# LayerNorm of the mix by thirds: tiles centred as they arrive, statistics on 88 rows, last mix tiles and first feed-forward products by thirds

## What is computed

```python
mix = (g_conv * y_conv + g_mla * y_mla) @ p['w_mix_out']
x1 = _layer_norm(DN_ALPHA * x + mix, p['ln1_g'], p['ln1_b'])
h, ffn_state = _causal_dwconv(ffn_prev, x1 @ p['w_up'], p['ffn_dw_w'], p['ffn_dw_b'])
hg, hv = jnp.split(h, 2, axis=-1)
f = (jax.nn.silu(hg) * hv) @ p['w_down']
y = _layer_norm(DN_ALPHA * x1 + f, p['ln2_g'], p['ln2_b'])
```

## Time and profile before

| | us |
|---|---|
| median of 3 runs | 2294.15 (2285.85 to 2295.95) |
| time of the profiled execution | 2278.77 |
| its span in the trace | 2276.9 |
| mean clock that TensorE was granted in it | 0.953 of full |
| TensorE busy | 2101.8 (92% of the span) |
| VectorE, ScalarE, GpSimd busy | 1324.0, 654.0, 443.0 |
| HBM traffic | 76 GB/s over the span |

### The profile page before, as it was taken

The page is one execution under the profiler, slowest core; times in us unless marked ns, Lnnn a source line. Parts: engine busy times, 40 slices in busy tenths (PEclk is TensorE's granted clock), DMA queues, the critical chain, the costliest instruction groups (busy, mean ns, idle before and its releaser), DMA issues.

```text
span 2276.9 us, 34903 instructions
## 1 busy us (share of the span) xinstructions
PE 2101.8 (92%) x13705; PEld 1989.7 (87%) x13705; DVE 1324.0 (58%) x1743; ACT 654.0 (29%) x1066; POOL 443.0 (19%) x230
## 2 busy tenths in 40 slices
PE   5999999969989999979989996799999999999992
PEld 5999999958979888866659995699999999999992
DVE  4799999964536666634433324855444454454545
ACT  3221222135224444433422102522222222222212
POOL 2222221101100010033311221121221222212213
PEclk6999999989979999989988997899999999999995
DMA  7222222215310000045624431011111111111102
GB/s 222 66 60 72 75 65 66 85 46 176 124 41 13 12 23 12 19 187 222 260 107 132 122 102 47 19 56 38 52 46 40 46 37 56 47 37 47 46 27 99
DMA packets 161092, 173.64 MB, mean 76 GB/s; under 512 B 19564, under 2 KB 136102, under 8 KB 156852
## 3 DMA queue, kind: packets, MB, share of 16 engines
q1 hardware_dynamic: 142805, 97.63, 14.6%
q0 software_dynamic: 8368, 46.27, 5.3%
q10 hardware_dynamic: 9825, 28.48, 3.4%
HBM read 145.48 MB, written 27.73 MB: 76 GB/s over the span
## 4 chain that ended last, share of the span: by engine, by line
PE 68%; issue 15%; DVE 12%; ACT 3%; DMA 1%; ACTq 1%; POOL 0%; DVEq 0%; POOLq 0%; SPq 0%
PE psb L1753 18%; PE psa L1753 18%; PE psb L2188 6%; PE psa L2188 6%; PE psb L1862 5%; PE psa L1862 4%; DVE pst L1262 4%; PE psb L2088 1%; PE pst L2067 1%; DMA xt_d<-xst 1%; PE psa L2035 1%; PE psb L2035 1%; PE pst L1932 1%; DVE ptl L1411 1%; PE psb L1767 1%
## 5 line engine op out<-in xcount | busy, mean ns | idle before, releaser
L1262 DVE SCALAR_TENSOR_TENSOR pst<-g_ext,wtap,pst 128x512 f32<-128x512 f32 x464 | 306.9, 745 | 0.0
L1179 POOL TENSOR_TENSOR wlo<-wraw,whi 128x1024 fp32r<-128x1024 f32 x64 | 173.3, 2720 | 637.8 <-ACT whi L1046 637.8
L1643 DVE TENSOR_SCALAR hg<-ueg,fwv,vec 128x1024 f32<-128x1024 f32 x22 | 17.9, 813 | 231.1 <-ACT ueg L1063 231.1
L1115 POOL TENSOR_TENSOR wlo<-wraw,whi 128x1024 fp32r<-128x1024 f32 x32 | 77.0, 2412 | 377.6 <-ACT whi L648 358.3
L1753 PE MATMUL psa<-x1h,whi 128*128 128x352 f32 x528 | 115.9, 328 | 18.2 <-DVE x1l L1618 16.6
L1121 POOL TENSOR_TENSOR wlo<-wraw,whi 128x1024 fp32r<-128x1024 f32 x32 | 77.3, 2417 | 270.4 <-ACT whi L682 270.3
L1753 PE MATMUL psa<-x1h,wlo 128*128 128x352 f32 x528 | 114.2, 324 | 0.0
L1753 PE MATMUL psb<-x1h,whi 128*128 128x352 f32 x528 | 114.2, 324 | 0.0
L1753 PE MATMUL psa<-x1l,whi 128*128 128x352 f32 x528 | 114.1, 324 | 0.0
L1753 PE MATMUL psb<-x1h,wlo 128*128 128x352 f32 x528 | 113.8, 323 | 0.0
L1753 PE MATMUL psb<-x1l,whi 128*128 128x352 f32 x528 | 113.7, 323 | 0.0
(11 more groups left out here) (423 smaller groups left out, 5245.2 us busy)
## 6 DMA issues: line engine op xcount, KB each, us to landing
wraw<-in_w_up SPq DMA_DIRECT2D x44, 512.0 KB, 3.7
wraw<-in_w_in SPq DMA_DIRECT2D x37, 512.0 KB, 3.8
wraw<-in_w_down SPq DMA_DIRECT2D x22, 512.0 KB, 3.5
gb_d<-stg ACTq DMA_DIRECT2D x8, 528.0 KB, 2.7
ga_d<-stg ACTq DMA_DIRECT2D x8, 528.0 KB, 2.7
gab<-ga_d ACTq DMA_DIRECT2D x8, 528.0 KB, 4.4
ma_d<-stg ACTq DMA_DIRECT2D x8, 528.0 KB, 2.9
tmp<-gb_d SPq DMA_DIRECT2D x8, 528.0 KB, 3.7
```

Of the source, the lines that this page charges most:

```text
L1115: nc.gpsimd.tensor_tensor(wlo[:, n % HL, :], wraw[:, n % RAW, :], whi[:, n % HL, :].bitcast(F32), ALU.subtract).then_inc(lo_done, 1)
L1179: nc.gpsimd.tensor_tensor(wlo[:, (ns + 2) % HL, :], wraw[:, (ns + 2) % RAW, :], whi[:, (ns + 2) % HL, :].bitcast(F32), ALU.subtract).then_ ...
L1262: half[x] = link(nc.vector.scalar_tensor_tensor(out=dst, in0=src, scalar=tap(k_), in1=pst[:, x, :], op0=ALU.mult, op1=ALU.add))
```

## The change

The LayerNorm of the mix is worked in another order:

- Behind mix1, VectorE adds `res` tiles 0 and 1 (`pair`); behind mix2, TensorE sums that over the partitions in three parts, ScalarE scales by 1/256. This shift, the mean of two tiles, is taken off every tile: for tiles 2 to 7 VectorE forms alpha * x - shift in `stg` before the mix tile is there (`shifted`), and the add out of PSUM then gives the centred tile. Sums (`s1`) and squares (`tmp`) are added up tile by tile; ScalarE's squares stand between its casts of weights.
- The 44 transposes of state rows move behind mix3.
- mix6 and mix7 are made by thirds of the tokens, 24 matmuls each, in the order 6, 7, 6, 7, 6, 7 (`third`).
- Statistics per third: `token_sums` makes 16 FP32 matmuls with the data as weights (128 x 88) and one column of ones, so that sum and square sum of 352 tokens lie on 88 partitions x 4 columns. VectorE and ScalarE compute mean, variance, root, reciprocal on 88 x 4. `spread` brings 1/sd and -mean/sd back to all partitions with 8 FP32 matmuls against the identity. The first two thirds' sums and spreads stand inside the thirds of mix6 and mix7, the third spread behind the first third of GATE0 and VAL0.
- Normalising is a multiply and an add on VectorE per tile and third; then gain, bias, high and low part as before, by thirds.
- GATE0 and VAL0 are made by thirds (`first_up`): per third, GATE0 then VAL0, first the 16 matmuls with the high activations, then the 8 with the low ones.
- On ScalarE the casts of the weights of GATE1 and VAL1 move in front of the last third. The scaling of `res` by alpha moves behind the convolutions of GATE0 (tiles 0 to 3) and VAL0 (tiles 4 to 7).

SyncE's order is not changed.

```diff
-            for m in range(MT):
+            for m in range(3):
                 hi(N4 + m + 2)
...
+            for c in range(3):
+                act.wait_ge(l1_p, PS[f"c{c}"])
+                step(f"c{c}", nc.scalar.activation(stat[:, part3(c)], pst[:, c % 2, 0:CH], ACT.Copy, scale=1.0 / (2 * P)))
+            for m in range(2):
+                act.wait_ge(l1_v, VS[f"d{m}"])
+                step(f"sq{m}", nc.scalar.activation(tmp[m][:, :], res[:, m, :], ACT.Square))
+            for m in range(2, 6):
+                hi(N4 + m + 3)
+                mixed(m)
+                act.wait_ge(l1_v, VS[f"q{m - 1}"])
+                step(f"sq{m}", nc.scalar.activation(tmp[0][:, :], res[:, m, :], ACT.Square))
...
+            hi(N5 + 1)
+            square(6, 0)
+            square(7, 0)
+            sums_root(0)
+            square(6, 1)
+            spread(0)
...
+            affine(1, 0)
+            affine(1, 1)
+            spread(2)
...
+            for k in range(2, MT):
+                affine(1, k)
+            for kind in (GATE0, VAL0):
+                ffn_hi("first", kind)
+            for k in range(MT):
+                affine(2, k)
...
+            def shifted(m):
+                dve.wait_ge(xt_in[m % 2], 16 * (m // 2 + 1))
+                step(f"y{m}", nc.vector.scalar_tensor_tensor(out=stg[m % 2][:, :], in0=stg[m % 2][:, :], scalar=ALPHA,
+                                                             in1=stat[:, :], op0=ALU.mult, op1=ALU.subtract))
...
+            for m in range(2, 6):
+                q, n = ring[f"mix{m}"]
+                dve.wait_ge(w_used, N4 + m + HL + 1)
+                dve.wait_ge(l1_v, VS[f"y{m}"])
+                nc.vector.tensor_tensor(split(res[:, m, :]), split(stg[m % 2][:, :]), acc(q), ALU.add).then_inc(free[q], 1)
+                mixed(m)
+                step(f"p{m}", nc.vector.tensor_tensor(s1[:, :], s1[:, :], res[:, m, :], ALU.add))
+                dve.wait_ge(l1_s, AS[f"sq{m}"])
+                step(f"q{m}", nc.vector.tensor_tensor(tmp[1][:, :], tmp[1][:, :], tmp[0][:, :], ALU.add))
+                shifted(m + 2)
...
+            def normalise(c, k):
+                x = res[:, k, part3(c)]
+                if k == 0:
+                    dve.wait_ge(l1_s, AS[f"br{c}"])
+                step(f"u{c}{k}", nc.vector.tensor_tensor(x, x, stat[:, part3(c)], ALU.mult))
+                dve.wait_ge(l1_v, VS[f"u{c}{k}"])
+                step(f"n{c}{k}", nc.vector.tensor_tensor(x, x, s1[:, part3(c)], ALU.add))
...
+            for c in (1, 2):
+                for k in range(MT):
+                    normalise(c, k)
+                    if k:
+                        low(c, k - 1)
+                low(c, MT - 1)
...
+            def token_sums(c):
...
+                for kind, parts in enumerate(((s1[:, :], res[:, 7, :]), (tmp[1][:, :], stg[1][:, :]))):
+                    for x in range(SUB):
+                        cols = slice(c * CH + x * ST, c * CH + (x + 1) * ST)
+                        for k, src in enumerate(parts):
+                            last = nc.tensor.matmul(pst[0:ST, 0, 480 + kind * SUB + x:481 + kind * SUB + x], src[:, cols],
+                                                    ones[:, 0:1], start=k == 0, stop=k == 1)
...
+            between = {(6, 1): (token_sums, 0), (7, 1): (spread, 0), (6, 2): (token_sums, 1), (7, 2): (spread, 1)}
+            for c in range(3):
+                for m in (6, 7):
...
+                    third(N4 + m, j, c, mgh, mgl, range(0, 3))
+                    if (m, c) in between:
+                        what, of = between[(m, c)]
+                        what(of)
+                    last = third(N4 + m, j, c, mgh, mgl, range(3, KT))
...
+            token_sums(2)
```

More of the change, by code:

```diff
@@ L1017, in _ @@
[L1017 to L1029, removed]
+            told = {}
@@ L1032, in ffn_hi @@
+            affine(0, 2)
+            affine(0, 3)
+            sums_root(1)
+            square(6, 2)
+            spread(1)
+            affine(0, 4)
+            square(7, 2)
+            affine(0, 5)
+            affine(0, 6)
+            affine(0, 7)
+            sums_root(2)
+            affine(1, 0)
+            affine(1, 1)
+            spread(2)
             def ffn_hi(g, kind):
@@ L1600, in _ @@
[L1600 to L1609, removed]
@@ new lines, in _ @@
+            last_mix(7, 1)
+            normalise(0, 2)
+            normalise(0, 3)
+            variance(1)
+            scales(1)
+            last_mix(6, 2)
+            add_sums(2)
+            normalise(0, 4)
+            last_mix(7, 2)
+            normalise(0, 5)
+            normalise(0, 6)
+            for k in range(6):
+                low(0, k)
+            normalise(0, 7)
+            variance(2)
+            low(0, 6)
+            low(0, 7)
+            scales(2)
+            for c in (1, 2):
[4 more added lines that the diff above has]
+                low(c, MT - 1)
@@ L1680, in dve_ffn @@
                         ffn_conv(g, kind)
+                        if g == "first" and kind == GATE0:
+                            scale_residual(range(0, MT // 2))
                     elif kind in (VAL0, VAL1):
                         ffn_conv(g, kind)
+                        if g == "first" and kind == VAL0:
+                            scale_residual(range(MT // 2, MT))
                         if g == "first":
@@ new lines, in spread @@
+            def spread(c):
+                pe.wait_ge(l1_v, VS[f"f{c}"])
+                for b, src in enumerate((s_rstd, s_nmr)):
+                    for x in range(SUB):
+                        last = nc.tensor.matmul(pst[:, b, x * ST:(x + 1) * ST], src[0:ST, x:x + 1].to_broadcast([ST, P]),
+                                                ident[0:ST, 0:ST], start=True, stop=True)
+                step(f"b{c}", last)
+            for m in range(6):
+                weighed(N4 + m, f"mix{m}", mgh, mgl, ml_done if m == 0 else None)
+                if m == 2:
+                    shift_sum()
+                if m == 3:
+                    state_rows()
@@ new lines, in _, with first_up @@
+            token_sums(2)
+            def first_up():
+                for c in range(3):
+                    for v, kind in enumerate((GATE0, VAL0)):
+                        n, ns = blk("first", kind)
+                        wh, wl = slot3(whi, ns), slot3(wlo, ns)
+                        if c == 0:
+                            pe.wait_ge(lo_done, n + (RAW + 1))
+                            pe.wait_ge(free[v], acc5("first", kind, v) + 1)
+                        out = psx[v][:, c, 0:CH]
+                        for k in range(KT):
+                            if v == 0:
+                                pe.wait_ge(l1_s, AS[f"h{c}{k}"])
+                            for w in (wh, wl):
+                                nc.tensor.matmul(out, w[:, k, :], x1h[:, k, part3(c)], start=k == 0 and w is wh, stop=False)
+                        for k in range(KT):
+                            if v == 0:
+                                pe.wait_ge(l1_v, VS[f"l{c}{k}"])
+                            last = nc.tensor.matmul(out, wh[:, k, :], x1l[:, k, part3(c)], start=False, stop=k == KT - 1)
+                        if c == 2:
+                            last.then_inc(w_used, 1)
+                    if c == 0:
+                        spread(2)
@@ L2196, in pe_ffn @@
                         down(g, kind)
-                    else:
-                        up(g, kind, l1_l if g == "first" and kind == GATE0 else None)
+                    elif g != "first" or kind in (GATE1, VAL1):
+                        up(g, kind)
+            first_up()
             pe_ffn("first")
```

244 lines of the change are left out of this document (191 added, 53 removed).

## The result

The changed kernel takes 2305.88 us, median of 8 runs (2301.19 to 2310.62); the kernel before 2289.11 (8 runs, 2285.2 to 2296.99, the three of the table above among them). The ratio is 1.0064, 95% interval 1.0049 to 1.0079: slower by 14.7 us (11.2 to 18.1), just over the 0.5% that this kernel's measurement can tell.

The account below looks back on a forecast made before the run. TensorE was taken to bound the kernel, dense from GATE1's start, so that start moves the end one for one: 10.2 us later, added to the runs' median 2294.15, gives 2304, range 2285 to 2318.

Parts of the forecast that it names:

- The loop of tiles 2 to 5: Mix tiles 2 to 5: a loop through the queues turns in 12.4 us; TensorE waits some 10 us before token sums.
- GpSimd's hold: GpSimd's low part, 2.4 us, counts in full in the mix loop, holding VectorE instructions that read two SBUF tiles.
- rival A: Mix loop: GpSimd does not hold VectorE, a turn takes 11.1 us and keeps up with TensorE; 2281.5 at best; chance 0.13.
- The thirds of the mix: Mix tiles 6 and 7 with first two token sums and spreads: 28.9 us from 1399.8, ending at 1428.7, not 1393.9.
- The thirds of GATE0 and VAL0: First two feed-forward products: VectorE leads at 1.43 us a tile, and work up to the last low part ends at 1471.0.
- TensorE's close: End of GATE0 and VAL0: 34 matmuls from 1470.5 and a fall of the clock, 5.5 + 1.65 us.
- Finish: Start of GATE1, the third feed-forward product: 1477.7 against 1467.5, 10.2 us later.
- B: TensorE's clock stays at 2.4 GHz but for the wait at 1389: 5.5 us less, 2299; chance 0.18.
- four falls: Drops of TensorE's clock to 1.2 GHz, priced at 1.65 us each, that a rival takes away for 5.5 us.
- C: Small FP32 matmuls on TensorE cost 0.216 us a pass at the low clock: 17 us more, 2321; chance 0.14.
- Beyond the finish: Behind GATE1's start: TensorE is dense, so a later start moves the end one for one.
- The slack of the first group: First feed-forward group: residual scalings on VectorE are hidden by GATE1 and VAL1, 21.1 us against TensorE's 23.3.

Follow-up runs that it names:

- a1: Changed kernel with ScalarE's squares of mix tiles 2 to 5 ahead of the casts of weights loaded behind the same add; ratio to the kernel before 1.0019.
- a6: Changed kernel with VectorE's add of mix tile 2 moved right behind its shifted x tile; ratio to the kernel before 1.0043.
- a2: Changed kernel with ScalarE's casts of the GATE1 and VAL1 weights moved ahead of its copies of the third spread; ratio to the kernel before 1.0042.
- c1: Changed kernel with 96 unused 16x16 transposes where TensorE waits for its first token sums; ratio to the kernel before 1.0050.
- d1: b1 with 96 unused 16x16 transposes in the second and third thirds of GATE0; ratio to the kernel before 0.9947.
- d2: Kernel before with 234 unused 16x16 transposes ahead of the second column sums; ratio to the kernel before 0.9996.
- a4: Kernel before with only the residual's scaling moved into VectorE's first feed-forward group; ratio to the kernel before 1.0012.
- b1: Changed kernel with squares of tiles 2 to 4 ahead of casts, two pairs of weight casts later, third spread between GATE0's and VAL0's first thirds; ratio to before 0.9951.
- a3: Changed kernel with each of the three groups of token sums issued twice over; ratio to the kernel before 1.0112.

## Why the prediction came out as it did

Times of after are given less 13.3 us, to stand beside those of the prediction.

- **The loop of tiles 2 to 5**: right in mechanism and size. Turn 12.4 forecast (its terms as listed add up to 12.5), 12.15 found; add of tile 5 ended at 1383.6 forecast, 1383.0 found; token sums at 1399.8, found 1399.6. a1 shows the order on ScalarE as its cause, a6 that its start counts in full.
- **GpSimd's hold**: right, shown by a2. The Trainium skill (SBUF — State Buffer, "SBUF: two separate sides"), weighed in the prediction, is borne out by the rows of 2.71 and 2.61 us, and rival A's loop of 11.1 us a turn did not come.
- **The thirds of the mix**: end at 1428.7 forecast, 1430.2 found. The mis-sized term is the token sums, 4.82 and 3.85 us instead of 3.2 each, because I gave one price a pass where there are two, by clock; the spreads, 1.77 and 1.75 for 2.1, gave 0.7 us back. The Trainium skill's 73 ns for 88 columns (TensorE: Matmul & The Clock Gate, "LDWEIGHTS") fits the pass of 0.078 at the high clock and not the 0.147 at the low one.
- **The thirds of GATE0 and VAL0**: end of the last low part at 1471.0 forecast, 1471.4 found; the third token sums at the high clock, 2.64 us for 3.2, and the spread had taken back 0.9 of the 1.5 us. ScalarE's wait for the third spread was 3.50 us, where I had named 4 to 5. TensorE's close took 7.7 us instead of 7.15. Finish 1477.7 forecast, 1478.6 found: 11.1 us later, for 10.2.
- **The rivals of the clock**: B (the clock stays high) did not come, with 0.77 and 0.75 granted in the two stretches behind the first token sums; its four falls at 1.65 us would be 6.6 us and not the 5.5 that I wrote. C had the mechanism right, since the low clock of the first group did not rise under such passes, and its price too high: 0.147 us a pass at 0.50, not 0.216. The three token sums took 11.3 us for 9.6.
- **Beyond the finish**: here a step failed. "From 1467.53 on TensorE is dense, so the later start of GATE1 moves the end one for one" left out that TensorE's program ahead of the loop had become longer: 2.6 us, which c1, d1 and d2 show to hang on that length. The kernel before carries such a price too, 2.3 us by d2. A wait of 1.7 us put down to "issue" was in its trace, and I did not ask what it was.
- **The slack of the first group**: counted 21.1 us against 23.3, with scalings at 1.2 us that cost 0.70 (a4). It had no effect, since the cover held either way. The Trainium skill would have told me (VectorE: DVE Perf Modes, "Mode 2×_2P — use both read ports for one tensor": an instruction that reads a single tile and has it and its output in SBUF uses both read ports, for two results a cycle); the 0.70 for 1056 columns, against 1.25 for one with two tiles, agrees.
- **The verdict**: the time forecast, 2304, is 2 us from the measured 2305.88, but that is luck: I started from 2294.15, the median of three runs, which is 5.0 above the 2289.1 of all eight, and the change costs 14.7 us where I had 10.2. The two errors cancel. Within 0.5% was my likeliest case and slower by more the next; it came out at 0.64% (0.49 to 0.79). Of the 4.5 us between 10.2 and 14.7, 2.6 are the rest behind GATE1 and 0.9 the stage; 1.0 lies between the profiles and the medians and stays open.

## What to carry to other kernels

When a change streams work tile by tile, draw the loop through all queues before pricing its parts: here one cast that stood ahead of a square on ScalarE (10.5 us by a1) and two weight preparations at a bad moment (3.8 by a2) cost more than the 11.1 us by which the stage had grown; with both and two more things moved (b1) the same idea takes 10.7 us off, 0.49% measured. Put GpSimd's work where VectorE waits anyway, and small matmuls between large ones, so that more of them run at the high clock. And when a program's length changes ahead of a loop, look at the instruction loads and the waits called "issue" inside it before you explain the rest by the edit.

## What I had not expected of the hardware

- The place of a loop in TensorE's program is worth 4 to 5 us in 812: 6 or 7 instruction packets and a rest of 807.0 to 807.5 at one length, 43 packets and 811.4 to 812.2 at another, 15 or 16 and 809.2 to 809.4 at a third.
- Small FP32 matmuls don't keep the clock: 16 of 88 columns by 1 take 2.5 us at 1.00 and 4.7 at 0.50, and a group of 32 matmuls that began at 1.00 ended at 0.50 (a3's third: rows of two passes take 0.29 us until 1441.2, 0.43 from 1441.6).
- A small transpose costs less with fewer columns of weights: 96 with 16 columns took 2.55 us in c1, 0.027 each, where the 44 of the state rows, with 128 columns, took 0.064 each, both at the high clock (1.00 and 0.98).
